# One decode step with attention, HGRN2 and a mixture of experts: gate blocks between the steps of the sample recurrence, and output, routing and tail tile by tile

## What is computed

```
m   = sigmoid(ga) * (o_nsa @ w_branch_a) + sigmoid(gb) * (o_hg @ w_branch_b)
out = m @ w_out
y   = y + g1 * rms_norm(out, norm_mix_post)
h   = rms_norm(y, norm_ffn_pre) * (1 + sc2) + sh2
y   = y + g2 * rms_norm(moe_ffn(h), norm_ffn_post)

hgrn2, a chunk:  o = (q * exp(b)) @ S + tril(...) @ v
                 S = exp(b_end) * S + (k * exp(b_end - b)).T @ v

moe_ffn:  logits = h @ w_router + b_router; the top 4 of 32 experts, softmax over them
          out += weight * (clamped_swiglu(h @ w_up[e] + b_up[e]) @ w_down[e] + b_down[e])
```

## Time and profile before

| | |
|---|---|
| time, median of 3 runs | 1718.34 us (1717.71 to 1719.27) |
| profiled execution | 1717.43 us, span 1715.7 us |
| PE busy | 1498.3 us, 87% |
| DVE busy | 379.5 us, 22% |
| ACT busy | 292.2 us, 17% |
| DMA | 527.59 MB, mean 308 GB/s |
| granted PE clock, mean | 0.917 of full speed |

### The profile page before, as it was taken

How to read it: one execution, slowest core, us unless ns; L and a number is a source line. 1 busy time by engine, 2 the same in 40 slices (tenths; PEclk the granted TensorE clock), 3 DMA queues, 4 the chain that set the end, 5 groups by cost and what they waited for, 6 DMA issues and landing times.

```text
span 1715.7 us, 21858 instructions
## 1 busy us (share of the span) xinstructions
PE 1498.3 (87%) x8288; PEld 661.2 (39%) x8289; DVE 379.5 (22%) x804; ACT 292.2 (17%) x543; POOL 84.0 (5%) x122
## 2 busy tenths in 40 slices
PE   5989989779977955999999999999998998999980
PEld 4554445458854532333333232333332232332220
DVE  6110014256613243101011001011110010010106
ACT  5000006435321010111111101111111011011110
POOL 1000003200000000000000000000000000000002
PEclk9999999878987966999999999999999999999995
DMA  9774664961164623996999999899999999999954
GB/s 276 236 262 152 232 236 145 286 223 45 50 179 165 247 99 146 399 417 259 412 417 419 419 416 419 349 417 419 418 417 419 417 419 418 417 419 417 418 223 156
DMA packets 139315, 527.59 MB, mean 308 GB/s; under 512 B 11553, under 2 KB 40633, under 8 KB 104258
## 3 DMA queue, kind: packets, MB, share of 16 engines
q1 hardware_dynamic: 128482, 482.83, 71.9%
q0 software_dynamic: 10784, 44.07, 7.6%
HBM read 499.87 MB, written 31.15 MB: 310 GB/s over the span
## 4 chain that ended last, share of the span: by engine, by line
PE 55%; DMA 20%; SPq 11%; DVE 7%; issue 3%; ACT 2%; DVEq 0%; POOLq 0%; ACTq 0%; POOL 0%
PE bank L1278 19%; DMA arena<-in_b_up 14%; SPq L630 9%; PE bank L1300 6%; PE bank L1130 4%; PE bank L739 3%; DMA arena<-in_w_in 3%; PE bank L954 2%; PE bank L955 2%; SPq L635 2%; PE bank L1272 2%; PE bank L1203 2%; DMA arena<-in_cache_cmp,arena 1%; PE bank L1191 1%; DMA arena<-in_w_ada 1%
## 5 line engine op out<-in xcount | busy, mean ns | idle before, releaser
L1278 PE MATMUL bank<-arena 128*64 128x512 f32 x2176 | 494.1, 613 | 0.0
L1278 PEld LDWEIGHTS bank<-arena 128*64 128x64 f32 x2176 | 156.1, 140 | 338.6 <-issue 338.6
L1300 PE MATMUL bank<-arena 128*64 128x512 f32 x1088 | 254.9, 622 | 0.0
L2079 DVE TENSOR_SCALAR arena<-bank 128x512 f32<-128x512 f32 x34 | 23.5, 692 | 836.7 <-PE bank L1278 836.7
L1300 PEld LDWEIGHTS bank<-arena 128*64 128x64 f32 x1088 | 77.6, 142 | 153.8 <-issue 153.8
L1590 ACT ACTIVATE arena<-arena 128x512 f32<-128x512 f32 x34 | 21.5, 631 | 525.9 <-DVE arena L2079 525.9
L1248 PE MATMUL bank<-arena 128*64 128x512 f32 (+1 forms) x420 | 103.2, 609 | 8.0 <-DVE arena L2069 8.0
L2156 POOL DMA_DIRECT2D slots<-arena x68 | 36.0, 530 | 1299.0 <-ACT arena L1597 1296.8
L1130 PE MATMUL bank<-arena 128*128 128x288 f32 x256 | 78.7, 460 | 14.3 <-DMA arena<-in_w_in 11.1
L1272 PE MATMUL bank<-arena 1*64 1x512 f32 x272 | 40.3, 664 | 37.1 <-DMA arena<-in_b_up 35.5
L1130 PEld LDWEIGHTS bank<-arena 128*128 128x128 f32 x256 | 53.0, 216 | 31.9 <-DMA arena<-in_w_in 12.8
(11 more groups left out here) (392 smaller groups left out, 1304.9 us busy)
## 6 DMA issues: line engine op xcount, KB each, us to landing
arena<-in_w_up SPq DMA_DIRECT2D x256, 1024.0 KB, 19.2
arena<-in_w_down SPq DMA_DIRECT2D x128, 1024.0 KB, 22.6
arena<-in_w_ada SPq DMA_DIRECT2D x12, 2048.0 KB, 10.8
slots<-arena POOLq DMA_DIRECT2D x2, 6400.0 KB, 36.9
arena<-in_w_in SPq DMA_DIRECT2D x6, 2048.0 KB, 13.6
slots<-arena POOLq DMA_DIRECT2D x68, 128.0 KB, 5.5
arena<-in_w_in SPq DMA_DIRECT2D x16, 512.0 KB, 4.1
arena<-in_w_out SPq DMA_DIRECT2D x1, 4096.0 KB, 16.5
```

The lines of the kernel that those rows point to most:

```text
L1278: last = mm(banks[part][SLOT * s:SLOT * s + SLOT, :], xcT[:, q], ring[pos][:, D * part + 512 * s:D * part + 512 * s + 512], start=False, s ...
L1300: last = mm(banks[4][SLOT * s:SLOT * s + SLOT, :], lhs, ring[pos][:, D * v + 512 * s:D * v + 512 * s + 512], start=False, stop=f == 7)
```

## The change

It has three parts.

- Gate blocks that found no place inside the prompt's steps (`LEFT`) are issued by hand between the steps of the sample recurrence on PE, their copy by ACT becomes `tanh(x/2)`, the factor 0.5 goes into the copies of both mixer outputs, and the merge uses `(1 + tanh) * product`. The heads of the sample go into four groups of 32 partitions of bank 5. `vm` is made later. SP loads s0 earlier and alternates gate pieces with branch weights; s0 begins 512 floats later in the arena, so that it no longer overlaps the prompt's state.
- The output projection takes the sample first; tile 0 uses banks 6 and 7, tile 1 banks 2 and 3. ACT squares and sums (`Square` with `accum_out`), from the banks where the data is there. Each tile runs through both norms, in the order sample, 0, 1. Each tile's router products follow its own transposes. Counts come before ranks and in one column; slots are computed for tiles together; the first one-hot is made from a short form, and `in_chunk`, `rowu`, the softmax weights and their diagonal `wdiag` are computed after it. ACT's exps come after its copies for the first chunk.
- In the tail one gather brings all 4 x 32 rows of the sample, and PE sums them with `wdiag`; eight gathers follow for tiles 0 and 1. ACT makes the first of the weighted terms and the squares. Each tile is stored by itself, the sample first.

The diff, cut to its core:

```diff
 PROMPT_STEPS = prompt_steps()
+_end = max(n for n, s in enumerate(PROMPT_STEPS) if s[0] not in ("gates", "gates_out"))
+INSIDE = [j for j in range(NGATE) if PROMPT_STEPS.index(("gates_out", (j,))) < _end]
+LEFT = [j for j in range(NGATE) if j not in INSIDE]
+PROMPT_STEPS = [s for s in PROMPT_STEPS if s[0] not in ("gates", "gates_out") or s[1][0] in INSIDE]
+ORDER = (2, 0, 1)
...
+        scr2 = view(n_t + 2 * D, D)
...
+            def load_gate(j):
                 if j >= 2:
                     sp.wait_ge(S("gate_ps"), j - 1)
                 sp.dma_start(gate_piece[j % 2], w_in[:, ZW + P * j:ZW + P * j + P].rearrange("(k p) c -> p k c", p=P)
                              ).then_inc(S(f"ld_gp{j % 2}"), 16)
+
+            for j in range(len(INSIDE) + 2):
+                load_gate(j)
...
             sp.wait_ge(S("state"), 2)
+            sp.dma_start(s0, A["state_hgrn"][0].rearrange("b h k v -> k (b h) v")).then_inc(S("ld_s0"), 16)
             sp.dma_start(O[8][0, 0].rearrange("h k v -> k h v"), state).then_inc(S("st_state"), 16)
-            sp.wait_ge(S("st_state"), 16)
+            load_gate(len(INSIDE) + 2)
             sp.wait_ge(S("p_pv"), len(UNITS))
             after(sp, "mod_w")
             sp.wait_ge(S("st_mod"), 16 * 20)
...
-            sp.dma_start(s0, A["state_hgrn"][0].rearrange("b h k v -> k (b h) v")).then_inc(S("ld_s0"), 16)
-            broadcast_rows(gate_rows, 0, "ld_gate")
...
+            for k in range(6):
+                load_branch(k)
+                if len(INSIDE) + 3 + k < NGATE:
+                    load_gate(len(INSIDE) + 3 + k)
+            broadcast_rows(gate_rows, 0, "ld_gate")
+            sp.wait_ge(S("gate_ps"), NGATE)
+            for k in range(6, 8):
+                load_branch(k)
             sp.wait_ge(S("s_state"), 8)
             sp.dma_start(O[9][0].rearrange("b h k v -> k (b h) v"), s0).then_inc(S("st_state"), 16)
-            sp.wait_ge(S("st_state"), 32)
             sp.wait_ge(S("ohT_ps"), 3)
             broadcast_rows(mod_rows[:, 0], 2 * D, "ld_modr")
             broadcast_rows(mod_rows[:, 1], D, "ld_modr")
+            sp.wait_ge(S("st_state"), 32)
             sp.dma_start(arena[:, wo_at:wo_at + 8 * D].rearrange("p (k n) -> p k n", n=D),
                          A["w_out"][0].rearrange("(k p) n -> p k n", p=P)).then_inc(S("ld_wo"), 16)
...
-                    sp.wait_ge(S("out_ps"), 3)
+                    sp.wait_ge(S("out_ps"), 5)
                 if n == 12:
                     sp.wait_ge(S("y1"), 3)
-                    after(sp, "lg_ps")
+                    sp.wait_ge(S("lg_ps"), 3)
...
+                for j in LEFT[first:past]:
+                    gate_block(j, 0)
+                    gate_block(j, 1)
+
+            def new_states(first, past):
+                for n in range(first, past):
+                    h, half = n // 2, n % 2
+                    if n >= 2:
+                        pe.wait_ge(S("s_state"), n - 1)
+                    mm(banks[n % 2][:], kh_s[0:NS, DK * h:DK * h + DK], vm[0:NS, 4 * half:4 * half + 4, DK * h:DK * h + DK],
+                       start=True, stop=True).then_inc(S("sst_ps"), 1)
+
             transposed_output()
             pe.wait_ge(S("hg_cp"), 2)
             hgrn_inputs(2)
...
+            gate_blocks(0, 1)
...
+            gate_blocks(1, 2)
...
+            head = lambda h: banks[5][NS * h:NS * h + NS, 0:DK]
...
-                c = slice(DK * h, DK * h + DK)
-                mm(banks[5][0:NS, c], att_s[0:NS, h], zc(2, "hi", 512)[:, c], start=True, stop=False)
-                for b in range(NB):
-                    last = mm(banks[5][0:NS, c], qep[:, h, NS * b:NS * b + NS], s0[:, HH * b + h], start=False, stop=b == NB - 1)
+                mm(head(h), att_s[0:NS, h], zc(2, "hi", 512)[:, DK * h:DK * h + DK], start=True, stop=False)
+            for b in range(NB):
+                for h in range(HH):
+                    last = mm(head(h), qep[:, h, NS * b:NS * b + NS], s0[:, HH * b + h], start=False, stop=b == NB - 1)
             last.then_inc(S("o_ps"), 1)
+            gate_blocks(2, 3)
...
+            pe.wait_ge(S("onT"), 2)
             after(pe, "vm")
...
+            new_states(0, 2)
+            gate_blocks(3, 4)
+            new_states(2, 4)
+            gate_blocks(4, 5)
+            new_states(4, 6)
+            gate_blocks(5, len(LEFT))
+            new_states(6, 8)
             hgrn_out(2, oh_s)
...
                 for j in range(4):
                     last = mm(banks[5][32 * j:32 * j + 32, 0:256], mT[:, k, TP:TP + NS], wo[k][:, 256 * j:256 * j + 256],
                               start=k == 0, stop=k == KD - 1)
             last.then_inc(S("out_ps"), 1)
...
+            for i in range(2):
+                for n in range(2):
+                    for k in range(KD):
+                        last = mm(banks[(6, 2)[i] + n][:], mT[:, k, P * i:P * i + P], wo[k][:, 512 * n:512 * n + 512],
+                                  start=k == 0, stop=k == KD - 1)
+                    last.then_inc(S("out_ps"), 1)
+
+            for n, i in enumerate(ORDER):
...
+                pe.wait_ge(S("h2T"), n + 1)
+                pe.wait_ge(S("ld_wr"), 32)
...
+                last.then_inc(S("lg_ps"), 1)
+
+            for n, i in enumerate(ORDER):
+                pe.wait_ge(S("mk"), n + 1)
+                last = mm(banks[1][0:E, 0:1], mk[0:ROWS[i], i], ones[0:ROWS[i], 0:1], start=n == 0, stop=n == 2)
+            last.then_inc(S("cnt_ps"), 1)
...
-            after(pe, "tab")
             pe.wait_ge(S("oneslot"), 1)
             dispatch()
             pe.wait_ge(S("xr"), 1)
             chunk_T()
+            after(pe, "tab")
...
 
+            after(pe, "wdiag")
+            pe.wait_ge(S("ld_gath2"), 16)
+            for n in range(2):
...
             def gates_out(j):
                 act.wait_ge(S("gate_ps"), j + 1)
-                nc.scalar.copy(gates[:, j], banks[7][:, 0:TP + NS]).then_inc(S("gate_out"), 1)
...
+            more_gates(0, 1)
...
+            more_gates(1, 2)
...
+            for h in range(HH):
+                last = nc.scalar.copy(oh_s[0:NS, h], banks[5][NS * h:NS * h + NS, 0:DK])
+            last.then_inc(S("oh_cp"), 1)
+            more_gates(2, len(LEFT))
             hgrn_rms(2, oh_s, osq_s)
...
+                    last = fn(scr[0:r], orow[0:r], ACT.Square, accum_out=sq2[0:r, i, 0:1])
+                else:
+                    for half in range(2):
+                        act.wait_ge(S("out_ps"), 2 * n + half)
+                        last = fn(scr[0:r, 512 * half:512 * half + 512], banks[(6, 2)[i] + half][:], ACT.Square,
+                                  accum_out=sq2[0:r, i, half:half + 1])
+                last.then_inc(S("sq2"), 1)
...
+                link(act, "act", fn(scr[0:r], src, ACT.Square, accum_out=ss[0:r, i:i + 1]))
+                fn(rt_[0:r, i:i + 1], ss[0:r, i:i + 1], ACT.Sqrt, bias=eps_t[0:r], scale=1.0 / D).then_inc(S("rms"), 1)
...
+            for n, i in enumerate(ORDER):
+                square_sums(n, i)
+                root(i, 3 + n)
+                if n == 2:
+                    rows_T_out(0, 2)
+                squares_then_root(x[0:ROWS[i], i], i, "y1", n + 1)
+            rows_T_out(1, 0)
+            rows_T_out(2, 1)
...
+            for i in ORDER:
                 r = ROWS[i]
-                act.wait_ge(S("top"), i + 1)
...
+                    after(act, "comb_ps")
+                    for half in range(2):
+                        last = fn(scr[0:r, 512 * half:512 * half + 512], banks[6 + half][0:r, :], ACT.Square,
+                                  accum_out=sq2[0:r, i, half:half + 1])
+                    last.then_inc(S("sq2"), 1)
+                    root(i, 6)
...
+                    for v in range(2):
+                        act.wait_ge(S(f"ld_gath{v}"), 64)
+                        fn(accr[:, v], gath[:, 4 * v], ACT.Copy, scale=wts[:, v, 0:1]).then_inc(S("acc0"), 1)
+                else:
+                    squares_then_root(accr[0:r, i], i, "acc", n)
...
-            V.tensor_tensor(vm[0:NS], zc(2, "hi", 512).unsqueeze(1).broadcast_to([NS, NB, 512]),
-                            C("bmask", NS).unsqueeze(2).broadcast_to([NS, NB, 512]), ALU.mult).then_inc(S("vm"), 1)
             link(dve, "dve", V.memset(qep, 0.0))
...
             V.tensor_tensor(att_s[0:NS], banks[4][0:NS, 0:P].rearrange("p (h t) -> p h t", h=HH),
                             C("bt32", NS).unsqueeze(1).broadcast_to([NS, HH, NS]), ALU.mult).then_inc(S("att"), 1)
...
+            hgrn_squares(2, oh_s, osq_s)
...
-            hgrn_norm(2, oh_s, osq_s)
+            hgrn_gated(2, oh_s)
...
-                V.tensor_tensor(ga, ga, banks[2 * (n % 2)][:, 0:TP + NS], ALU.mult)
-                link(dve, "dve", V.tensor_tensor(gb, gb, banks[2 * (n % 2) + 1][:, 0:TP + NS], ALU.mult))
+                V.scalar_tensor_tensor(ga, ga, 1.0, banks[2 * (n % 2)][:, 0:TP + NS], ALU.add, ALU.mult)
```

(46 more changed lines are left out.)

283 lines of the change are left out of this document (131 added, 152 removed).

## The result

The changed kernel takes 1649.45 us (median of 4 runs, 1644.51 to 1650.68); the kernel before took 1718.03 us beside it (4 runs, 1716.39 to 1719.27). The ratio is 0.9596, with a 95% interval of 0.9575 to 0.9617. The forecast was 1652.0 us in a range of 1643 to 1668.

What follows compares the result with a forecast made beforehand. The weight stream paces the expert loop, while chains of small steps bound the stretches before and after it. Savings of 27.5 + 30.5 + 7.9 = 65.9 us from 1717.4 gave 1651.5, forecast 1652 us, range 1643 to 1668.

Steps and rivals of the forecast that it cites:

- The loop moves rigidly: Expert loop: with the ring full at its start as before, it shifts earlier whole, its length unchanged at about 1003 us.
- Part 1: Sample recurrence before the merge: gate blocks between its steps start the merge at 515.5 instead of 543.03, 27.5 us less.
- Heads don't overlap: Rival, sample recurrence's heads: weight loads overlap matmuls only where the row group differs, so 1658 us; chance 0.05.
- Blocks 12 to 15 wait for no DMA: Sign, gate blocks in the sample recurrence: their weight pieces, landing 3.9 us after issue, arrive before they are needed.
- Part 2: Output projection to routing: the first dispatch starts at 57.4 us instead of 88.3, 30.9 less, of which 30.5 is taken.
- the added links: Output projection to first dispatch: allowance for extra chain steps, lowering the 30.9 us gain to 30.5.
- a third of the 8.03: Routing: tile 1's share of the 8.03 us of router products, in the chain from h2 at 40.7 to logits at 47.6.
- Part 3: Tail after the expert loop: last store issued 8.9 us earlier, larger store about 1.0 longer, 7.9 us less.
- Clock: Rival, interleaved gate blocks: half fall to 1.2 GHz and cost 3 x 4.2 us more, 1665 us; chance 0.12.
- Pieces late: Rival, gate pieces sharing the queue with s0, store and branch loads: three blocks wait 4 us, 1664 us; chance 0.08.
- Tables: Rival, prompt stage on ACT: tanhs between exps reload tables, 25.6 us, about half on the chain, 1665 us; chance 0.03.
- Slower ring: Rival, expert loop: transfers to the weight ring, moved 384 bytes up, are slower, each per cent costing 10 us; chance 0.03.

Runs made afterwards that it cites:

- e11: The changed kernel run once more with no edit; ratio 0.9614 to the kernel before.
- e3: Changed kernel with the sample recurrence's head products back in one group of 32 partitions, with one copy out; ratio 0.9654 to the kernel before.
- e4: Changed kernel with the six gate blocks in one row ahead of the sample recurrence, on PE and ACT; ratio 0.9755 to the kernel before.
- e10: Changed kernel plus four moves: earlier sample norm, earlier tile 0 transpose copies, tail reordered with early root table, later state store; median 1639.76 us, ratio 0.9574.
- e7: Changed kernel with gate blocks in one row, heads in the old places and the old tail, keeping the second part and tanh; ratio 0.9843.
- e12: Changed kernel with e10's moves, but the last gate block one step earlier and the tail order restored, root table still loaded early; ratio 0.9592.
- e8: Changed kernel with the six sums of squares between output projection and routing on VectorE again; ratio 0.9614 to the kernel before.
- e9: Changed kernel with the work behind the output projection in two loops over all tiles instead of tile by tile; ratio 0.9625.
- e5: Changed kernel with sigmoid instead of tanh as the gate's function, constants adapted; ratio 0.9621 to the kernel before.
- e1: Changed kernel with its ring of weight buffers 384 bytes lower, where the kernel before had it; ratio 0.9607 to the kernel before.
- e2: Kernel before the change with only its ring of weight buffers moved 384 bytes higher; ratio 1.0008 to the kernel before.
- e6: Changed kernel with the old tail: twelve gathers, weighted sums and squares on VectorE, prompt tiles stored together and first; ratio 0.9647.

## Why the prediction was right

**The bound.** Every stretch ahead of the loop passed to the end whole: the loop was neither shortened nor lengthened beyond its spread, and the DMA share in it is 0.99 as in the earlier trace rows. "The loop moves rigidly" held within about 1 us in the mean. (The two rows lie 31.22 us apart, not 31.24; nothing rests on it.)

**Part 1, forecast 27.5, measured 29.5** (merge at 513.53, forecast 515.5). That it is this near is in part luck: the stretch from first Ln to merge holds the prompt stage, which spreads over 6 us, and e11 would give 34.3. Counted from the second attention transposes, 44.3 us and 27.6 of blocks before became 43.0, which is 28.9. PE's queue from 469.2 took 40.3 us instead of 42.0. Inputs 3.6 as forecast. The heads took 2.2 (483.17 to 485.41), not 4.0: this is the mis-sized term. I took 0.055 us for each of 72 matmuls from a row with 256 columns; with 128 they start every 0.031 us (1.96 us for 64), so a row with the right number of columns was wanted. Scores and keys took 0.8 instead of 1.7, at the higher clock now. The blocks took more, because block 10 ran 5.57 us at a partly lower clock. State products 7.6 as forecast, and from their end to the merge 4.0 instead of 4.4. In e3 and e4 the two halves of this part measured 5.3 and 25.7 us by undoing them, 31.0 together, more than the part gained; undoing the interleaving alone also uncovers the wait for piece 12, which the kernel before did not have.

The sentence of the Trainium skill on the heads (TensorE: Matmul & The Clock Gate, "Part 3: Packing small matmuls": weight loads overlap only where the row group differs) does not hold here. In the source lines above, each with all 128 rows and one of four column groups, a load takes 108 ns and yet 64 loads and 64 matmuls lie within 1.96 us, one pair every 31 ns. In e3, with a single column group, sixteen pairs take 1.94 us, one every 121 ns. So loads overlap the matmuls, and each other, where only the column group differs. Within one group the pace is the same in both, a pair every 121 to 124 ns; it is the four groups that run beside each other. And loads run beside matmuls even where no group differs: in the gate blocks, which use the whole array, sixteen loads fill 3.71 of the 4.16 us in which their sixteen matmuls run.

```profile
485.41 3.71 PEld L1153 LDWEIGHTS bank<-arena 128*128 128x128 f32 x16 [0.21 <-DMA arena<-in_w_in]
```

The rival "Heads don't overlap" falls with it.

**Queues.** "Blocks 12 to 15 wait for no DMA" was nearly right: block 12 waited 0.21 us in the profiled execution, and 1.0 to 1.4 in those with its order of loads in which block 10 ran fast. Two things were not priced. The piece does not land after 3.9 us as in the earlier trace rows: from its issue to block 12 it took 7.0 us (478.45 to 485.41), 7.4 in e4, 7.7 in e10 and 8.8 in e7, beside s0, the state's store and the branch loads. And between s0 and this load stands the state's store, left out of my order, whose issue holds SP for 5.5 to 6.7 us; with the load ahead of it the wait went from 1.0 to 1.4 us down to 0.39 (e10) and 0.45 (e12). Without the interleaving both together leave a wait of 4.8 to 6.0 us (e4, e7).

**Part 2, forecast 30.5, measured 30.6.** Right within 0.2 us, partly because errors met. By the chain's own marks, from the start of the sample's projection: last half 31.4 (forecast 31.9), y1 35.5 (36.3), h2 39.8 (40.7), logits 48.2 (47.6), choice 50.3 (49.7), dispatch 57.65 (57.8 with the added links). h2 came 0.9 us early, 0.5 of them from the projection; from h2 to the logits it took 8.4 us and not 6.9. Tile 0's logits stood in front on PE; e10 and e12 show that wait by taking it away: 1.4 us. And the router products of tile 1 took 3.6 us, not "a third of the 8.03", since the sample's sixteen are far shorter (0.69 us in this trace) and a prompt tile's take nearly half; 1.2 us of my 6.9 that no named term fills covered that. From 585 to 606 the granted clock is 0.50, as it was 0.54 in this stretch before; at the higher clock the same sixteen products took 1.97 us (tile 0 in e10). What that clock costs the whole routing was not tried. The sums on ScalarE are 0.5 us (e8), running tile by tile is 5.9 (e9).

**Part 3, forecast 7.9, measured 8.7** (8.8 in the mean over all executions). Gather 6.7 us (forecast 6.4, though 10.33 less three times 1.27 is 6.5), products 3.6 (3.5), squares 1.2 (1.5), load and root 1.6, weighted sums and residuals as forecast. The last store is issued 9.4 us earlier (8.9), and the two stores cost 0.7 us more (1.0).

**Rivals.** Clock: not as priced, since only block 10 ran slow (5.57 us, 5.76 in e8, at a granted clock of 0.73 and 0.71), and in the eight other executions with the interleaving none of the six did. Pieces late: at most 1.4 us instead of 12. Tables: no reload, and no price (e5). Slower ring: nothing that stands out of the loop's spread (e1, e2).

## What to carry to other kernels

Before moving an operation to another engine, ask which tile's chain is left at the end of the stretch: finishing the early tiles under the last one's matmuls was worth twelve times as much here as moving their sums (5.9 against 0.5 us). When an idle time is taken away, look for what is issued by the same event that ended the work before it (a buffer freed, a store in front of a load), since that is the next wait. And compare such edits by the stretch that they touch: output projection to dispatch repeated within 0.05 us between executions whose totals differed by several us.

## What the runs showed of the hardware

- Two executions of the same kernel, perhaps on two chips, differ by 5.7 us in span, most of it in the prompt's attention and HGRN2 stage (first Ln to attention transposes: 138.35 and 133.39 us, and 133.4 to 139.3 over the twelve executions of the changed kernel and its variants). On one chip (e5 to e8) that stage took 138.1 to 139.3, on two others 133.4 to 137.1. The expert loop spreads over 6.4 us, 1000.98 to 1007.41, with 1002.3 to 1005.9 on the first of these chips alone. What causes either spread stays open.
- Nineteen more table loads (24.4 us of ACT) left the merge within 0.7 us of a run with the tanh on the same chip (e5 against e6).
- Matmuls of 128 columns and 32 output rows, in turn into four groups of 32 partitions, start every 31 ns at 2.4 GHz, each with a weight load of its own.
- The first matmuls of the merge run at 1.2 GHz in every execution: the first eight take 3.6 to 4.2 us, also in e12, where PE had been idle for only 0.84 us in one piece and not 3.00. The second eight take 2.11 us in six of the fourteen executions and 2.28 to 3.18 in the other eight, before and after the change; all later ones take 2.11. So taking PE's idle time away did not bring the higher clock to the merge.
- A gather landed 6.7 us after its issue, as the first of a row (1616.80 to 1623.50) or as the fifth, issued 1.24 us behind the fourth (1610.64 to 1617.32 in e10). So a row of gathers is paced by POOL's issues, and the last one's landing cannot be hurried by what is done with the first.
